# Splitting the expert rows straight from x in its own column order, with a strided stationary operand in the gather

## The reference, cut to what matters

```python
h = h + hierarchical_moe(rmsnorm(h, norm_ffn), w_router_group, w_router_expert, w_gate, w_up, w_down)
# rmsnorm(x, g) = x * rsqrt(mean(x * x) + EPS) * g        g = norm_ffn: one gain per column

# hierarchical_moe, t = the 256 normed rows:
group_logits = t @ w_router_group                 # softmax and argmax over 8 groups
exp_logits = t @ w_router_expert                  # within the group: the two best of 8 experts
gate = softmax(top_logit) * p_group
# for each expert e, on the rows xb routed to it:
hid = silu(xb @ w_gate[e]) * (xb @ w_up[e])       # 1024 -> 512
y   = hid @ w_down[e]                             # 512 -> 1024, times gate, added to the row's token
```

## Time and profile before

| | |
|---|---|
| median of 3 runs | 1627.99 us |
| the profiled execution's own time | 1625.19 us |
| its span, first to last instruction | 1623.1 us |
| TensorE busy (matmul) | 1491.2 us, 92% of the span |
| VectorE / ScalarE / GpSimd busy | 560.9 / 462.5 / 37.7 us |
| DMA | 489.21 MB, mean 301 GB/s |
| chain that ended last, by engine | PE 61%; DMA 16%; DVE 5%; ACT 2% |

### The profile page before, as it was taken

The page is one execution under the profiler, slowest core; times in us unless marked ns, Lnnn a source line. Parts: engine busy times, 40 slices in busy tenths (PEclk is TensorE's granted clock), DMA queues, the critical chain, the costliest instruction groups (busy, mean ns, idle before and its releaser), DMA issues.

```text
span 1623.1 us, 20165 instructions
## 1 busy us (share of the span) xinstructions
PE 1491.2 (92%) x7961; PEld 936.4 (58%) x7963; DVE 560.9 (35%) x878; ACT 462.5 (28%) x761; POOL 37.7 (2%) x43
## 2 busy tenths in 40 slices
PE   7999979999999988969999889889889989999996
PEld 5897869988889967744434334334333433444342
DVE  5754566554474867541111101101111111111112
ACT  5535635543465673331111101101111011111111
POOL 1000000000020000220000000000000000000000
PEclk9999989999999988989999999999999999999998
DMA  8464335554544321769999999999999999999993
GB/s 302 159 221 143 104 125 172 191 179 166 200 127 160 104 104 53 289 270 424 414 420 427 428 430 427 428 431 427 428 431 427 428 430 376 416 426 413 421 412 126
DMA packets 80284, 489.21 MB, mean 301 GB/s; under 512 B 6431, under 2 KB 8611, under 8 KB 56804
## 3 DMA queue, kind: packets, MB, share of 16 engines
q1 hardware_dynamic: 79044, 484.17, 74.1%
q0 software_dynamic: 1184, 4.26, 0.8%
HBM read 506.21 MB, written 1.08 MB: 313 GB/s over the span
## 4 chain that ended last, share of the span: by engine, by line
PE 61%; DMA 16%; DVE 5%; ACT 2%; issue 1%; SPq 1%; DVEq 0%; ACTq 0%
PE bank L1271 22%; PE bank L874 19%; DMA slots<-in_w_up_dram 15%; PE bank L1307 9%; PE bank L1241 4%; PE bank L1251 2%; DMA slots<-in_w_down_dram 1%; ACT w_split L566 1%; DVE w_split L1397 1%; PE bank L864 1%; PE bank L936 1%; SPq L410 1%; DVE xeT L1869 1%; PE bank L1181 1%; PE bank L1171 0%
## 5 line engine op out<-in xcount | busy, mean ns | idle before, releaser
L1271 PE MATMUL bank<-slots,xeT 128*64 128x512 f32 x1536 | 353.6, 616 | 47.5 <-DMA slots<-in_w_up_dram 47.4
L1271 PEld LDWEIGHTS bank<-slots,xeT 128*64 128x64 f32 x1536 | 119.2, 142 | 276.9 <-issue 276.9
L1397 DVE TENSOR_TENSOR w_split<-raw,w_split 128x2048 fp32r<-128x2048 f32 (+2 forms) x98 | 209.8, 2171 | 82.8 <-ACT w_split L566 82.8
L1307 PE MATMUL bank<-slots,heT 128*64 128x512 f32 x1024 | 226.8, 595 | 8.3 <-ACT heT L810 7.0
L874 PE MATMUL bank<-w_split,h_hi 128*128 128x512 f32 (+1 forms) x672 | 207.0, 390 | 4.0 <-DVE w_split L1397 2.3
L874 PE MATMUL bank<-h_hi,w_split 128*128 128x256 f32 x1120 | 207.8, 285 | 2.1 <-DVE w_split L1397 2.1
L566 ACT ACTIVATE w_split<-raw 128x2048 fp32r<-128x2048 f32 (+2 forms) x98 | 174.6, 1818 | 62.5 <-PE bank L874 56.3
L874 PEld LDWEIGHTS bank<-h_hi,w_split 128*128 128x128 f32 x1120 | 176.7, 192 | 4.2 <-DVE w_split L1397 2.5
L1878 DVE TENSOR_TENSOR h_e<-bank,h_e 128x512 f32<-128x512 f32 x32 | 22.1, 692 | 430.0 <-PE bank L1271 430.0
L874 PE MATMUL bank<-h_lo,w_split 128*128 128x256 f32 x560 | 158.8, 284 | 0.0
L1307 PEld LDWEIGHTS bank<-slots,heT 128*64 128x64 f32 x1024 | 71.1, 137 | 145.3 <-issue 133.1
(11 more groups left out here) (313 smaller groups left out, 1389.5 us busy)
## 6 DMA issues: line engine op xcount, KB each, us to landing
slots<-in_w_up_dram SPq DMA_DIRECT2D x64, 2048.0 KB, 18.9
slots<-in_w_down_dram SPq DMA_DIRECT2D x64, 2048.0 KB, 15.2
areas<-in_w_gate_dram SPq DMA_DIRECT2D x32, 2048.0 KB, 14.2
slots<-in_w_gate_dram SPq DMA_DIRECT2D x32, 2048.0 KB, 20.4
raw<-in_w_in_dram SPq DMA_DIRECT2D x42, 1024.0 KB, 5.5
raw<-in_w_ff_dram SPq DMA_DIRECT2D x32, 1024.0 KB, 5.3
raw<-in_w_out_dram SPq DMA_DIRECT2D x12, 1024.0 KB, 5.2
raw<-in_w_ple_gate_dram SPq DMA_DIRECT2D x4, 1024.0 KB, 5.2
```

The lines of the kernel that those rows point to most:

```text
L1271: last = mm(bank[SLOTS * e:SLOTS * e + SLOTS, :], xeT[:, k, odd, SLOTS * e:SLOTS * e + SLOTS], expert_panel(w, e, odd)[:, k, :], start=(k ...
L1307: last = mm(banks[half][SLOTS * e:SLOTS * e + SLOTS, :], heT[:, c, SLOTS * e:SLOTS * e + SLOTS], expert_panel("down", e, odd)[:, c, 512 * ...
L1397: last = tt(lo, source, hi, ALU.subtract)
```

## The change

The gain `norm_ffn_2` is no longer multiplied into the rows. It is loaded as one small column block (`moe_gain`, 8 values per partition) and applied when the gather's banks are emptied. With that, `t_hi` is made by one ScalarE instruction per 128 tokens straight from `x`, in the column order of `x`, and `t_lo` by one VectorE instruction, also from `x`. GpSimd does none of it. Since the rows keep the order of `x`, the gather's stationary operand for tile k is every eighth column (`by_column`). Each bank is now emptied by two instructions with a per-partition gain. For the first pass, the gather takes all products with `t_hi` first and those with `t_lo` after them, and VectorE makes `t_lo` after the token counts and does the rest of the routing (gate values) after emptying the first gather. The diff, cut to its core:

```diff
@@ -164,6 +164,7 @@
         neg_sink = sb("neg_sink", [P, HEADS])
+        moe_gain = sb("moe_gain", [P, KT])
@@ -211,9 +212,8 @@
 
-        t_all = rows_area(1)
         zeros = area(4)[:, 0:256].bitcast(mybir.dt.bfloat16)
-        gains = rows_area(5)
+        final_gain = area(5)[:, D:2 * D]
@@ -234,6 +234,10 @@
+
+        def by_column(row):
+
+            return row.rearrange("t (p k) -> t k p", k=KT)
@@ -494,25 +498,13 @@
             pool.wait_ge(y_gated, 1)
-            pool.dma_start(gains[:, 0, :], norm_ffn_2.to_broadcast([P, D])).then_inc(gains_loaded, 16)
-            pool.dma_start(gains[:, 1, :], norm_final.rearrange("(a n) -> a n", a=1).to_broadcast([P, D])).then_inc(gains_loaded, 16)
+            pool.dma_start(moe_gain[:, :], norm_ffn_2[0].rearrange("(p k) -> p k", k=KT)).then_inc(gains_loaded, 16)
+            pool.dma_start(final_gain, norm_final.rearrange("(a n) -> a n", a=1).to_broadcast([P, D])).then_inc(gains_loaded, 16)
...
-
-            pool.wait_ge(gains_loaded, 32)
-            for half in range(2):
-                pool.wait_ge(x_ready, X_OUT1 + 2 * half + 2)
-                for m in range(MT):
-                    to, row, gain = (v.rearrange(order, k=KT)[:, :, 64 * half:64 * half + 64]
-                                     for v, order in ((t_all[:, m, :], "t (k p) -> t k p"), (x[:, m, :], "t (p k) -> t k p"),
-                                                      (gains[:, 0, :], "t (p k) -> t k p")))
-                    nc.gpsimd.tensor_tensor(to, row, gain, ALU.mult).then_inc(t_made, 1)
-            for m in range(MT):
-                pool.wait_ge(t_rounded, m + 1)
-                nc.gpsimd.tensor_tensor(t_lo[:, m, :], t_all[:, m, :], t_hi[:, m, :].bitcast(F32), ALU.subtract).then_inc(t_ready, 1)
@@ -788,16 +780,18 @@
             for m in range(MT):
-                act.wait_ge(t_made, 3 + m)
-                link(act_(t_all[:, m, :], t_all[:, m, :], ACT.Copy, scale=stats[:, 8 + m:9 + m]))
-                act_(t_hi[:, m, :], t_all[:, m, :], ACT.Copy).then_inc(t_rounded, 1)
+                act_(t_hi[:, m, :], x[:, m, :], ACT.Copy, scale=stats[:, 8 + m:9 + m]).then_inc(t_rounded, 1)
+            act.wait_ge(gains_loaded, 32)
...
                 act.wait_ge(gathered, 4 * couple + 2 * half + 1)
-                act_(xeT[:, 4 * half:4 * half + 2].rearrange("p k o s -> p (k o s)"), banks[bank][:, :], ACT.Copy).then_inc(xe_a, 1)
+                for k in (4 * half, 4 * half + 1):
+                    last = act_(xeT[:, k].rearrange("p o s -> p (o s)"), banks[bank][:, S * (k % 2):S * (k % 2) + S], ACT.Copy,
+                                scale=moe_gain[:, k:k + 1])
+                last.then_inc(xe_a, 1)
@@ -1232,16 +1226,22 @@
 
-            def gather(couple, half, first_bank=0):
+            def gathering(half, first_bank, parts_of_t):
...
                     for k in range(4 * half + 2 * b, 4 * half + 2 * b + 2):
-                        for m in range(MT):
-                            for t in (t_hi, t_lo):
-                                last = mm(banks[first_bank + b][:, S * (k % 2):S * (k % 2) + S], t[:, m, P * k:P * k + P],
+                        for t in parts_of_t:
+                            for m in range(MT):
+                                last = mm(banks[first_bank + b][:, S * (k % 2):S * (k % 2) + S], by_column(t[:, m, :])[:, k, :],
                                           pick_r[:, m, :, :].rearrange("p e s -> p (e s)"),
-                                          start=(m == 0 and t is t_hi), stop=(m == 1 and t is t_lo))
-                    last.then_inc(gathered, 1)
+                                          start=(m == 0 and t is t_hi and k % 2 == 0), stop=(m == 1 and t is t_lo and k % 2 == 1),
+                                          skip_group_check=True)
+                    if t_lo in parts_of_t:
+                        last.then_inc(gathered, 1)
+
+            def gather(couple, half):
+
+                gathering(half, 0, (t_hi, t_lo))
@@ -1312,9 +1312,13 @@
                 pe.wait_ge(picked, first + 1)
-                gather(first, 0)
+                pe.wait_ge(t_rounded, MT)
+                gathering(0, 0, (t_hi,))
                 pe.wait_ge(marks_done, 1)
-                gather(first, 1, 2)
+                gathering(1, 2, (t_hi,))
+                pe.wait_ge(t_ready, MT)
+                gathering(0, 0, (t_lo,))
+                gathering(1, 2, (t_lo,))
@@ -1331,8 +1335,6 @@
 
-            pe.wait_ge(t_rounded, MT)
-            pe.wait_ge(t_ready, MT)
@@ -1828,11 +1830,21 @@
 
-            def finish_routing():
+            def count_tokens():
...
+
+            def rest_of_t():
+
+                for m in range(MT):
+                    dve.wait_ge(t_rounded, m + 1)
+                    stt(t_lo[:, m, :], x[:, m, :], stats[:, 8 + m:9 + m], t_hi[:, m, :].bitcast(F32),
+                        ALU.mult, ALU.subtract).then_inc(t_ready, 1)
+
+            def finish_routing():
@@ -1866,7 +1878,10 @@
                 dve.wait_ge(gathered, 4 * couple + 2 * half + 2)
-                copy(xeT[:, 4 * half + 2:4 * half + 4].rearrange("p k o s -> p (k o s)"), banks[bank][:, :]).then_inc(xe_d, 1)
+                for k in (4 * half + 2, 4 * half + 3):
+                    last = ts(xeT[:, k].rearrange("p o s -> p (o s)"), banks[bank][:, S * (k % 2):S * (k % 2) + S],
+                              moe_gain[:, k:k + 1], None, ALU.mult)
+                last.then_inc(xe_d, 1)
@@ -1893,9 +1908,12 @@
             choose(0, 0, True)
-            finish_routing()
+            count_tokens()
+            rest_of_t()
+            dve.wait_ge(gains_loaded, 32)
...
             gather(0, 1, 3)
+            finish_routing()
@@ -1928,7 +1946,7 @@
             for m in range(MT):
-                stt(xn[:, m, :], x[:, m, :], stats[:, 8 + m:9 + m], gains[:, 1, :], ALU.mult, ALU.mult).then_inc(out_ready, 1)
+                stt(xn[:, m, :], x[:, m, :], stats[:, 8 + m:9 + m], final_gain, ALU.mult, ALU.mult).then_inc(out_ready, 1)
```

More of the change, by code:

```diff
@@ L275, in program @@
         y_gated, att_ready, wo2_done = sem("y_gated"), sem("att_ready"), sem("wo2_done")
-        t_made, t_rounded, t_ready, routed, route_max, route_exp, marks_ready, ranks_made, marks_done = (
-            sem("t_made"), sem("t_rounded"), sem("t_ready"), sem("routed"), sem("route_max"), sem("route_exp"), sem("marks_ready"), sem("ranks_made"), sem("marks_done"))
+        t_rounded, t_ready, routed, route_max, route_exp, marks_ready, ranks_made, marks_done = (
+            sem("t_rounded"), sem("t_ready"), sem("routed"), sem("route_max"), sem("route_exp"), sem("marks_ready"), sem("ranks_made"), sem("marks_done"))
         pair_landed = {(w, e): sem(f"{w}{e}_landed") for w in ("gate", "odd_gate", "up", "down")
```

## The result

The changed kernel takes **1654.16 us** (median of 5 runs, 1649.69 to 1659.96), beside 1626.98 us for the kernel before in the same session. The ratio is 1.0168 (95% interval 1.0146 to 1.0189): slower by 27 us, where 3 us faster was forecast and 1636.8 us was the upper end of the range. Run again at the end of the study it gave 1.0182 (1.0161 to 1.0202).

A forecast was written before the change was run, and what follows sets the result against it. The expert half was taken as bound by a load stream whose start the first gate product sets. Terms -4.28 + 1.14 + 0 = -3.14 us took the median 1627.99 to 1624.9 us; range 1622.9 to 1636.8.

The forecast's parts named there:

- the upper end: Strided gather loads at full price: 62 ns per matmul, +11.9 us, 1636.8 us; rival's chance 0.25.
- the stationary operand with a stride of eight columns: Gather's 32 strided weight loads per gather: taken as +0, with +11.9 us over 192 matmuls at the other end.
- the rule of 16 bytes: At the gather's strided loads: each access into a new 16-byte line pays a penalty; no price stated.
- nearest in kind: L1285's strided loads within a flow of short matmuls, pitch 0.123 us, used to price the gather's stride at 0.
- How many gathers count: Gathers where added TensorE time reaches the end: the start and five, at 750, 802, 1329, 1381 and 1486 us.
- the lock: In the routing, GpSimd's work holds VectorE through a shared port pair; removing it brings the first gather 4.28 us forward.
- what the rest of the change is worth: Whole kernel with the stride priced at 0: -4.28 + 1.14 + 0 = -3.14 us.
- emptying in two pieces: VectorE's bank emptying behind gathers: +0.19 us each, +1.14 in all; TensorE's bank wait 0.36 us, not 0.17.
- the new order of the first pass: First gather does 16 t_hi products first, leaving nearly no wait for t_lo; price 0, bound 0 to 1.1 us.
- The clock rival: At the first gather, shorter TensorE idling keeps its clock up; about 1623.8 us, chance 0.07.

The follow-up runs named there:

- turns_probe: reorder_scaled plus 32 transposes of x at strides 1, 2, 4, 8 behind the router product, and L1285's transposes reading neighbouring columns; 1623.12 us, one execution.
- reorder_pool_back: reorder with two GpSimd subtracts of 1024 columns put back, their result unused; 1627.68 us, ratio 1.0013 to the kernel before.
- group2: Changed kernel with columns stored in groups of two tiles, so the gather's stationary operand has stride 2; 1624.11 us, ratio 0.9979 to the kernel before.
- reorder_scaled: Changed kernel, but ScalarE writes scaled rows in tile order, then rounds to t_hi; VectorE subtracts and gather reads neighbouring columns; 1623.48 us, ratio 0.9982.
- reorder: Changed kernel, but ScalarE and VectorE write t_hi and t_lo in tile order, so the gather reads neighbouring columns; 1625.88 us, ratio 0.9993.
- kept_warm: reorder_scaled with 32 transposes of x added behind the router product into an unread bank; 1622.76 us, ratio 0.9966 to the kernel before.

## Why the prediction was wrong

- **The step that failed** is the last term of the sum, "the stationary operand with a stride of eight columns". I took 0 and put the upper end at 62 ns a matmul. It is 121 ns. I priced a product's load by a transpose's, because both had a pitch of 0.12 us; but the transpose has only half the price to pay (turns_probe), and its pitch with neighbouring columns was 0.11, so it had room where the gather had none. The upper end came from the same wrong row. The 62 ns are what a transpose's load grows by; a product's load grows by 145 ns, of which 121 reach the pitch. In both kinds the pitch grew by less than the duration, so the way to the bound held here, and what failed is the load it was read from.
- The lines on the rule of 16 bytes spoke against the change. I gave the row that was "nearest in kind" more weight, though its operation was of another kind.
- **How many gathers count.** I took the start and five; the account shows the start and six: once TensorE's couples are 4 us longer, the gather at 1434 us, which I had left out, stands ahead of dry loads as well. The forecast's own arithmetic with 0.121 us and seven gathers gives -3.14 + 0.19 + 224 x 0.121 = +24.2 us, beside +24.8 in the profiles, of which 1.9 lie ahead of the change: 22.9 are left to explain. So it is near, but not right in its parts. At the start the gather loses 1.98 us and not 3.87, since its matmuls were slow already at the granted clock of 0.50.
- **Right: the lock.** -4.28 us forecast, -4.32 in the trace. With two subtracts alone reorder_pool_back puts 3.85 of it back.
- **Right: what the rest of the change is worth.** Without its stride of eight the change gains what was forecast for it: group2 0.9979 and reorder_scaled 0.9982, about -3.4 and -2.9 us, against -3.14. The intervals are some 2 us wide to either side, so the nearness is more than these runs can show.
- **Right: emptying in two pieces.** TensorE's wait for the bank is 0.34 us in place of 0.17; 0.36 was forecast.
- **Right: the new order of the first pass hides `t_lo`.** Without it the gate product comes 2.9 us later. But with the longer, strided `t_lo` of reorder the cover was too short.
- **The clock rival** was rightly held unlikely: the granted clock is 0.60 over 704 to 712 us in the changed kernel. That keeping it up is worth 1.8 us at the start was shown by kept_warm.

## What to carry to other kernels

Before a reordering pass is traded for a strided stationary operand, count the 16-byte lines that a load of 128 columns touches: with two fp32 of each line it was free, with one it cost 0.12 us per load of a product, and behind a moving operand of 256 columns nothing hid it at the full granted clock. A pass can be moved off a slow engine and still leave pairs of neighbouring columns together, as group2 does. And look at GpSimd's instructions for what stands beside them: 5 us of its work held VectorE's chain for 4.

## What the runs showed of the hardware that I had not expected

- The price of a stride is not the same for both kinds of weight loads: 0.12 us more pitch for an fp32r product, 0.01 us more for a transpose with the same 128 columns.
- The strided load has a pitch of 0.25 us at a granted clock of 0.50 as well as 0.24 at 1.00, while the load of neighbouring columns goes from 0.21 to 0.12. So the stride costs little where the clock is low.
- Useless transposes ahead of a gather brought the first gate product 1.8 us forward, with the granted clock at 1.00 in place of 0.50.
- A stride of eight on one of the two 1024-column operands that a VectorE operation reads took it from 1.24 to 2.07 us (reorder), and ScalarE's from 1.1 to 2.1 us.
